# The second norm and the first four up units of a two-block network, computed by halves of the tokens

## The reference, cut to what matters

```python
yx = token_mixers(hx @ w_in, ...)                      # 1024 channels per token
x = x + gt1 * rmsnorm(yx @ w_out, g_post_mix)
hx = modulate(rmsnorm(x, g_pre_ffn), sh2, sc2)         # h * (1 + scale) + shift
u, gate = jnp.split(hx @ w_up, 2, axis=-1)             # 2816 channels each
u = dwconv_grid(u, w_cf, b_cf, rows, width)            # 3 x 3 taps over 8 x 64 tokens
x = x + gt2 * rmsnorm((jax.nn.silu(u) * gate) @ w_down, g_post_ffn)
```

## Time and profile before

| | before |
|---|---|
| median of 3 runs | 1467.69 us |
| profiled execution | 1468.28 us, span 1466.5 us, mean granted clock 0.97 |
| PE busy | 1389.0 us (95%), 6923 matmuls |
| DVE busy | 887.4 us (61%) |
| POOL busy | 834.2 us (57%) |
| ACT busy | 398.6 us (27%) |
| chain that ended last | PE 81%, DVE 10%, issue 4%, ACT 2% |

### The profile page before, as it was taken

The page is one execution under the profiler, slowest core; times in us unless marked ns, Lnnn a source line. Parts: engine busy times, 40 slices in busy tenths (PEclk is TensorE's granted clock), DMA queues, the critical chain, the costliest instruction groups (busy, mean ns, idle before and its releaser), DMA issues.

```text
span 1466.5 us, 19722 instructions
## 1 busy us (share of the span) xinstructions
PE 1389.0 (95%) x6923; PEld 1119.9 (76%) x6923; DVE 887.4 (61%) x1271; ACT 398.6 (27%) x757; POOL 834.2 (57%) x651
## 2 busy tenths in 40 slices
PE   5898889999699999999999999999799999999998
PEld 4677667878478888888877888766588888888887
DVE  5678688764666666650018698744674888887000
ACT  3430323332332222220013203254522233232000
POOL 1233343435566666667775577433266777777665
PEclk9899999989899999999998999999999999999999
DMA  9358312112123333323332233211032333333332
GB/s 354 125 186 295 93 43 59 58 44 72 44 72 99 90 98 100 96 84 104 93 100 74 82 86 99 75 44 48 25 101 87 100 100 92 94 100 93 90 93 83
DMA packets 224459, 142.05 MB, mean 97 GB/s; under 512 B 5611, under 2 KB 211088, under 8 KB 224400
## 3 DMA queue, kind: packets, MB, share of 16 engines
q1 hardware_dynamic: 223509, 140.65, 31.9%
q10 hardware_dynamic: 891, 0.58, 0.1%
HBM read 139.12 MB, written 2.10 MB: 96 GB/s over the span
## 4 chain that ended last, share of the span: by engine, by line
PE 81%; DVE 10%; issue 4%; ACT 2%; POOL 1%; DMA 1%; SPq 0%; DVEq 0%; POOLq 0%; ACTq 0%
PE ps L547 24%; PE ps L549 24%; PE ps L548 24%; DVE ada_acc L1761 2%; PE ps L836 2%; DVE norm_acc L1674 1%; DMA v_tok<-in_w_ada 1%; DVE SS L1944 1%; PE ps L1077 1%; PE ps L1093 1%; PE ps L1106 1%; ACT h_hi L1187 1%; POOL w_lo L510 1%; DVE xT L2112 1%; DVE norm_t L1688 0%
## 5 line engine op out<-in xcount | busy, mean ns | idle before, releaser
L510 POOL TENSOR_TENSOR w_lo<-raw,w_hi 128x1024 fp32r<-128x1024 f32 x213 | 534.2, 2508 | 17.8
L547 PE MATMUL ps<-h_hi,w_hi 128*128 128x512 f32 x1064 | 428.0, 402 | 11.1 <-DVE h_lo L1695 6.9
L549 PE MATMUL ps<-h_hi,w_lo 128*128 128x512 f32 x1064 | 419.7, 394 | 0.0
L548 PE MATMUL ps<-h_lo,w_hi 128*128 128x512 f32 x1064 | 419.5, 394 | 0.0
L506 POOL TENSOR_TENSOR w_hi<-raw,cst 128x16 fp32r<-128x16 f32 x213 | 61.6, 289 | 584.9 <-PE ps L549 521.4
L547 PEld LDWEIGHTS ps<-h_hi,w_hi 128*128 128x128 f32 x1064 | 203.0, 191 | 63.4 <-issue 17.2
L549 PEld LDWEIGHTS ps<-h_hi,w_lo 128*128 128x128 f32 x1064 | 202.7, 190 | 43.9
L548 PEld LDWEIGHTS ps<-h_lo,w_hi 128*128 128x128 f32 x1064 | 203.2, 191 | 40.2
L507 POOL TENSOR_SCALAR w_hi<-raw 128x1008 fp32r<-128x1008 f32 x213 | 232.4, 1091 | 0.0
L2033 DVE SCALAR_TENSOR_TENSOR f_acc<-ps,par,f_acc 128x441 f32<-128x441 f32 (+2 forms) x176 | 122.3, 695 | 50.2 <-ACT f_acc L1187 27.9
L547 PE MATMUL ps<-f_hi,w_hi 128*128 128x512 f32 x352 | 138.3, 393 | 0.2 <-POOL w_lo L510 0.2
(11 more groups left out here) (291 smaller groups left out, 1920.8 us busy)
## 6 DMA issues: line engine op xcount, KB each, us to landing
raw<-in_w_up SPq DMA_DIRECT2D x88, 512.0 KB, 3.7
raw<-in_w_in SPq DMA_DIRECT2D x59, 512.0 KB, 3.8
raw<-in_w_down SPq DMA_DIRECT2D x32, 512.0 KB, 3.6
v_tok<-in_w_ada SPq DMA_DIRECT2D x18, 512.0 KB, 6.1
ada_first<-in_w_ada SPq DMA_DIRECT2D x8, 1024.0 KB, 10.2
raw<-in_w_out SPq DMA_DIRECT2D x16, 512.0 KB, 3.6
ada<-in_w_ada SPq DMA_DIRECT2D x14, 512.0 KB, 5.6
raw<-in_w_down SPq DMA_DIRECT2D x16, 384.0 KB, 3.3
```

The lines of the kernel that those rows point to most:

```text
L510: pool.tensor_tensor(w_lo[:, slot % 2, :], raw[:, slot, :], w_hi[:, slot % 2, :].bitcast(F32), ALU.subtract).then_inc(S("lo_split"), 1)
L547: nc.tensor.matmul(dst, lhs_hi, rhs_hi, start=first, stop=False)
L548: nc.tensor.matmul(dst, lhs_hi, rhs_lo, start=False, stop=False)
L549: return nc.tensor.matmul(dst, lhs_lo, rhs_hi, start=False, stop=last)
```

## The change

Norm 3 becomes two norms, `k` = 3 for tokens 0 to 255 and `k` = 4 for tokens 256 to 511 (later norms are numbered one higher), and both go the way of the other norms: one-column matmuls (`sum_tile`), reciprocal of 128 x 2, spread over PSUM, from which DVE reads it. POOL no longer adds residuals nor makes low parts. The first four up units run over the first half of the tokens, then over the second. So that all four stay in place, two extra places `w_more_hi`/`w_more_lo` hold units 33 and 34; before that they hold units 29 and 30, whose split no longer waits for units 27 and 28 but for the last attention output (`outputs_mm`).

```diff
-                    [("mo", [P, KT, T], F32)])
+                    [("w_more_hi", [P, 2, 1024], F32R), ("w_more_lo", [P, 2, 1024], F32R), ("mo", [P, 1, T], F32)])
...
+    def place_free(u):
+        if FIRST["out_g"] <= u < FIRST["out_g"] + 2:
+            return S("outputs_mm"), CHUNKS
+        if FIRST["out_g"] + 2 <= u < FIRST["up"] + 4:
+            return S("units_done"), u - 3
+        return S("units_done"), u - 1
...
-        stream(4, FIRST["up"] + 2)
-        residual_odd()
-        low_odd()
-        stream(FIRST["up"] + 2, UNITS)
+        stream(4, FIRST["out_g"])
+        for u in range(FIRST["out_g"], FIRST["up"] + 4):
+            split(u, u % 4, 16 * (u // 4 + 1), unit_place(u))
+        stream(FIRST["up"] + 4, UNITS)
...
+        def sum_tile(k, m):
+            cols = token_cols(k)
+            pe.wait_ge(S("norm_squared"), KT * k + m + 1)
+            tiles = range(cols.start // P, cols.stop // P)
+            for t in tiles:
+                mm = nc.tensor.matmul(ps[:, 7, cols.start + t:cols.start + t + 1], norm_sq[:, m % 2, t * P:(t + 1) * P], const("mean"),
+                                      start=(m == 0 and t == tiles[0]), stop=(m == KT - 1), skip_group_check=True)
+            mm.then_inc(S("norm_ss" if m == KT - 1 else "square_used"), 1)
...
-        spread(2, T, "rinv_spread")
-        sum_tiles(3, (S("rinv_ready"), 3))
+        for half in range(2):
+            if half:
+                pe.wait_ge(S("rinv_ready"), 3)
+            else:
+                pe.wait_ge(S("norm_inverted"), 3)
+            for t in range(2 * half, 2 * half + 2):
...
+            mm.then_inc(S("rinv_spread"), 1)
+        pe.wait_ge(S("rinv_ready"), 4)
+        for m in range(KT):
+            sum_tile(3, m)
+        spread(3, T, "rinv_ready")
+
+        def up_pair(half, u, banks, between=lambda at: None):
+            cols = (FIRST_HALF, SECOND_HALF)[half]
+            for at in range(KT + 4):
+                between(at)
+                for n in range(2):
+                    k = at - 4 * n
+                    if k < 0 or k >= KT:
+                        continue
+                    if half == 0 and k == 0:
+                        wait_unit(u + n)
+                    if n == 0:
+                        pe.wait_ge(*h_done(2 + half, k))
+                    hi, lo, slot = unit_place(u + n)
+                    mm = triple(ps[:, banks[n], cols], hi[:, slot, k * P:(k + 1) * P], lo[:, slot, k * P:(k + 1) * P],
+                                h_hi[:, k, cols], h_lo[:, k, cols], k == 0, k == KT - 1)
+                    if k == KT - 1 and half == 1:
+                        mm.then_inc(S("units_done"), 1)
+        def second_sums(at):
+            if 1 <= at <= 4:
+                sum_tile(4, 2 * at - 2)
+                sum_tile(4, 2 * at - 1)
+        up_pair(0, f, (0, 1))
+        up_pair(0, f + 2, (2, 3), second_sums)
+        spread(4, T, "rinv_ready")
+        up_pair(1, f, (0, 1))
+        up_pair(1, f + 2, (2, 3))
...
-        gated_residual(2, 0, 0, mo[:, 0, :], 1)
-        invert(3)
-        modulated(3, 2, lambda m: xT[:, m, :], lambda m: scale_in[:, 2, m:m + 1], lambda m: mod[:, 24 + m, 0:1], h_hi, h_lo)
+        gated_residual(0, range(KT))
+        dve.wait_ge(S("rinv_ready"), 4)
+        gated_residual(1, range(4))
+        new_modulated(0)
+        gated_residual(1, range(4, KT))
+        new_modulated(1)
```

More of the change, by code:

```diff
@@ L370, in build_program, with more_slot, unit_place @@
     KEPT = MIX_BANKS.index(7)
+    def more_slot(u):
+        return next((u - f for f in (FIRST["out_g"], FIRST["up"]) if f <= u < f + 2), None)
+    def unit_place(u):
+        return (w_hi, w_lo, u % 2) if more_slot(u) is None else (w_more_hi, w_more_lo, more_slot(u))
+    def place_free(u):
[4 more added lines that the diff above has]
+        return S("units_done"), u - 1
     HEAD_PARTS = [slice(0, QH // 2), slice(QH // 2, QH), slice(QH, NQK)]
@@ L1197, in square @@
             acc, buffers = squares_of(k)
-            dst = buffers[:, m % 2, 0:n]
+            cols = token_cols(k, n)
+            dst = buffers[:, m % 2, cols]
             if k in TILED:
@@ L1426, in _, with copy_rinv, new_squares, new_shifted @@
             activate(yg_hi[:, h, :], oT[:, h, :], ACT.Copy).then_inc(S("y_hi_ready"), 1)
-        def post_squares(k, wait, kept, bank):
+        def copy_rinv(k, dst):
+            act.wait_ge(S("rinv_spread"), {6: 3, 7: 4}[k])
+            activate(dst, ps[:, stat_bank(k), :], ACT.Copy).then_inc(S("rinv_ready"), 1)
+        def new_squares(half):
+            k, cols = 3 + half, (FIRST_HALF, SECOND_HALF)[half]
             for m in range(KT):
-                square(k, m, lambda m: ps[:, bank(m), :], wait)
-                if k == 4 or m == KEPT:
-                    activate(kept[:, m if k == 4 else 0, :], ps[:, bank(m), :], ACT.Copy).then_inc(S("mo_copied"), 1)
+                square(k, m, lambda m: xT[:, m, cols], lambda m: act.wait_ge(*x_done(half, m)))
             root(k)
-        def copy_rinv(k, dst):
-            act.wait_ge(S("rinv_spread"), {2: 1, 5: 2, 6: 3}[k])
-            activate(dst, ps[:, stat_bank(k), :], ACT.Copy).then_inc(S("rinv_ready"), 1)
+        def new_shifted(half):
+            for m in range(KT):
+                shifted(2 + half, m, h_hi, lambda m: mod[:, 24 + m, 0:1], (FIRST_HALF, SECOND_HALF)[half])
         act.wait_ge(S("y_ready"), 8)
-        post_squares(2, lambda m: act.wait_ge(*out_ready(m)), mo, lambda m: MIX_BANKS[m])
-        copy_rinv(2, norm_rinv[:, :])
-        def modulate(k, i, shift, residual):
-            for m in range(KT):
-                square(k, m, lambda m: xT[:, m, :], lambda m: act.wait_ge(*x_done(residual, m)))
-            root(k)
-            for m in range(KT):
-                shifted(i, m, h_hi, shift)
-        modulate(3, 2, lambda m: mod[:, 24 + m, 0:1], 0)
+        for m in range(KT):
+            square(2, m, lambda m: ps[:, MIX_BANKS[m], :], lambda m: act.wait_ge(*out_ready(m)))
+            if m == KEPT:
+                activate(mo[:, 0, :], ps[:, MIX_BANKS[m], :], ACT.Copy).then_inc(S("mo_copied"), 1)
+        root(2)
+        for half, cols in enumerate((FIRST_HALF, SECOND_HALF)):
+            act.wait_ge(S("rinv_spread"), half + 1)
+            activate(norm_rinv[:, cols], ps[:, 7, cols], ACT.Copy).then_inc(S("rinv_ready"), 1)
+        for half in range(2):
+            new_squares(half)
+            new_shifted(half)
         def ffn_pair(i, up, j, s, n):
@@ L1489, in _ @@
         load_sqrt(0)
-        post_squares(4, lambda m: act.wait_ge(*down_ready("down", m)), mo2, lambda m: (m + 7) % 8)
         for m in range(KT):
-            act.wait_ge(*x_done(1, m))
+            square(5, m, lambda m: ps[:, (m + 7) % 8, :], lambda m: act.wait_ge(*down_ready("down", m)))
+            activate(mo2[:, m, :], ps[:, (m + 7) % 8, :], ACT.Copy).then_inc(S("mo_copied"), 1)
+        root(5)
+        for m in range(KT):
+            act.wait_ge(*x_done(2, m))
             activate(h_hi[:, m, :], xT[:, m, :], ACT.Copy, scale=column("attn_norm_2", m)).then_inc(S("h_hi_ready"), 1)
         for m in range(KT):
-            square(5, m, lambda m: xT[:, m, :], lambda m: act.wait_ge(*x_done(1, m)))
+            square(6, m, lambda m: xT[:, m, :], lambda m: act.wait_ge(*x_done(2, m)))
         def head_squares(i):
```

235 lines of the change are left out of this document (113 added, 122 removed).

## The result

The changed kernel takes 1473.16 us in the median of 5 executions (1469.78 to 1478.82), the kernel before 1467.62. The ratio is 1.0049, with a 95% interval of 1.0032 to 1.0066. Run again beside the first experiments it was 1476.1 against 1468.02, ratio 1.0059 (1.0034 to 1.0084). The forecast was 1471.5 and slower. Sign and range hold for the first of these medians; the second lies 0.6 us above the range. Both terms of the sum stand at the places that were named, and both have the wrong size. The executions of the changed kernel lie far apart (1469.78 to 1481.88 us in the two sessions), those of the kernel before less so (1461.88 to 1470.12).

What follows compares the result with a forecast made beforehand. PE bounds most of the program, but DVE, ACT and POOL in turn bound 377.4 to 398.8 us. Terms 2.7 + 1.1 = 3.8 us on 1467.7 gave 1471.5 us; range 1464.5 to 1475.5, the forecast's own 1469.5 to 1473.5.

Steps and rivals of the forecast that it cites:

- Both terms of the sum: Unit 37 starting 2.7 us later, plus a 1.1 us PE wait ahead of 375: 3.8 us slower.
- Port wait ahead of 375: Early POOL splits hold up DVE's first low part after attention, so PE waits 1.1 us.
- the third rival: POOL's next split gets in between DVE's low parts, making them 1.3 to 3.6 us later; chance 0.13.
- upper bound of 4.7: Largest PE wait ahead of 375, if POOL's next split also gets in between the four low parts.
- Stage from the sum to unit 37: From the norm's sum through the up pairs: unit 37 starts at 428.7, 2.7 us later than 426.01.
- first `h` product: First 256-column up product, on the first token half, expected near 391, with `h` 7.7 us earlier than before.
- second pair: Second pair of up units on the first half: after 400.2, sixteen products of 5.8 us plus sums, ending 409.6.
- four groups of sums: Norm 4's eight one-column passes, four times, in the second pair: 0.9 us each, 3.6 in all.
- gap: PE idle of 1.6 us between the token halves, waiting for the second half's first low part.
- wait for L533: PE waits about 2.3 us ahead of unit 37 for its low split.
- lower clock behind the gap: Granted clock falls to about 0.5 after PE's idle between the halves, costing 0 to 3.1 us; 1.0 taken.
- Cover behind unit 37: In the up loop, taps stay ahead of PE by 2.5 us at unit 39, so no cost.

Runs made afterwards that it cites:

- e1: Changed kernel with the splits of units 31 and 32 waiting as before the change; 1477.37 us, ratio 1.0062 to the kernel before.
- e2: Changed kernel with only the split of unit 32 waiting as before, unit 31 still split early; 1477.17 us, ratio 1.0071 to the kernel before.
- e10: e9 with unit 35 finished before unit 36 begins in the second half (eight products apart, not four); 1466.59 us, ratio 0.9996 to the kernel before.
- e8: e6 plus extra places for units 37 and 38, and second half's squares added on VectorE, spread at step 11; 1469.89 us, ratio 1.0027.
- e9: e8 with units 37 and 38 in ordinary places again, sum and spread at steps 6 and 8; 1463.41 us, ratio 0.9977 to the kernel before.
- e5: Changed kernel with the split of unit 31 waiting until the four low parts are made; 1473.52 us, ratio 1.0046 to the kernel before.
- e3: Changed kernel with the second half's norm spread two steps before the end of the second pair; 1470.63 us, ratio 1.0027 to the kernel before.
- e6: Changed kernel with the edits of e5 and e3 together; 1471.18 us, ratio 1.0023 to the kernel before.

## Why the forecast was near, and which terms were off

*Port wait ahead of 375: forecast 1.1 us, measured 5.6* (mark to sum, 30.20 - 24.62). This is the step that failed. The rule cited there from the Trainium skill ("SBUF — State Buffer", "Who interferes with whom") was right, by these traces too: the first low part took 2.13 us and ended at 353.25, 0.56 behind the end of POOL's instruction, and the first product waited 1.01 us where 1.1 was worked out. Wrong was what I drew from POOL's 128 x 16 instruction that "let two of DVE's pass": it did stand back in that row (it came at 353.44 and ended at 354.23, behind the fourth low part at 354.15), but I took from this one row that POOL gives way, and the low parts behind the first as free. In the changed kernel the two engines take turns, one instruction each. That was the third rival, priced at 1.3 to 3.6 us and given 0.13; e1 and e2 show it, for the waits go with the splits. Neither the forecast nor the rival had the lower clock behind the three waits, 2.2 us, so the upper bound of 4.7 was too low as well.

*Stage from the sum to unit 37: forecast 2.7 us, measured 52.10 - 51.11 = 1.0.* The parts, less the 4.7 us by which the sum came late: first `h` product 391.6 (forecast 391.1); second pair begins 399.2 (400.2: the clock was back 3.4 us behind the first product, not 7); four groups of sums 0.885 each (0.9); VectorE scales from 409.2 (410.2); gap 1.64 (1.6), then the lower clock (0.67 in 415 to 420 us, forecast to fall); POOL's start 423.2 (425.0); the wait for L533 2.09 (2.3); unit 37 at 427.0 (428.7). All mechanisms were there. Of the error of 1.7 us, 1.0 is the clock's earlier return (1.5, less the 0.5 by which the first `h` product was late). The lower clock behind the gap cost 0.7 where 1.0 was taken, and unit 35 ended earlier ahead of its pair than the 1.2 us taken.

*Cover behind unit 37: forecast no cost, measured 0.2 us.* Right for this kernel, but the turns were priced from rows in which `f_lo` took 0.69 us, and it now takes 1.72. A gain of 1.1 us at unit 37 makes the loop 5 us longer (e10: 345.70, against 340.6 to 340.8 where the clock stayed up).

The first term was 4.5 us too small and the second 1.7 too large, which makes 6.6 of 3.8. So it is in part luck that the first median lies 1.7 us from the forecast: the two errors have opposite signs, and the distances up to the norm alone would give 1467.6 + 6.8 = 1474.4 us, which is the third rival's time (1472.8 to 1475.1) and above the forecast's own 1469.5 to 1473.5. The medians differ by 5.5 and 8.1 us instead of 6.8; that this is how the clock falls in later gaps rests on the two traces alone.

What was only argued: that it is the one-column groups which let the clock fall in a busy stream. Three kernels without them (e8, e9, e10) kept it up to the second half, of eight traces with them three did; no run moved them alone to another place in the list. Why a first group 3.1 to 3.8 us behind the clock's return gives the lower clock, and one 4.3 to 4.7 us behind it does not, stays open.

## What to carry to other kernels

Work that an extra buffer lets run ahead lands on other engines' work: before splitting early, look at what VectorE does in that stretch with two operands in SBUF, and hold the early work back by one wait if needed. Here the wait won 5.2 us up to unit 33, of which the clock took 4.6 back (e5). Check the cover of the loop behind a stage with the durations that the new overlap gives, not those of the old trace: a start 1.1 us earlier made the loop 5 us longer. And compare by marks inside the program over several traces, since 4.3 of the 6.8 us lost here were hidden by chance in the one profiled execution.

## What the runs showed of the hardware

- VectorE instructions with both inputs in SBUF and GpSimd's splits alternated one by one: four of 0.63 us took 6.96 beside GpSimd's 2.73, 0.66, 1.47 and 2.68, and GpSimd's own of 1.03 and 2.37 grew to 1.47 and 2.73 (changed kernel). VectorE's with an operand in PSUM kept 0.48 us beside the splits (e1).
- TensorE's granted clock fell to 0.5 in a stretch with 8.00 us busy of 8.00, behind a stream with three groups of eight one-column matmuls (e5), the first of them 3.4 us behind the clock's return; with the same instructions and 4.6 us in place of 3.4 it did not (changed kernel). The cost was 4.6 us.
- A wait of TensorE of 2.1 us ahead of unit 37 was followed by the lower clock in e1 (0.72 in 433 to 439) and e9 (0.72 in 422 to 428), and not in the changed kernel, e3 and e6.
